# The low-part subtraction of a dense weight unit on GpSimd, as four instructions of 512 columns

## The chip, the cores and the metric

The kernel runs on one core of a Trainium2 chip. The metric is the device time of one execution in microseconds; the time before is 525.37 us, the median of three runs (525.44, 525.37, 520.17). Durations in the text come from one profiled execution, which took 521.39 us and whose span in the trace is 519.6 us. TensorE is the matrix engine (PE in the profile), VectorE is DVE, ScalarE is ACT, GpSimd is POOL, and SyncE (SP) issues most of the DMAs. SBUF is the on-chip memory of 128 partitions, PSUM the eight banks into which TensorE writes.

## What is computed

One layer of a hybrid decoder on 256 tokens of width 1024, all in float32:

```python
mod = silu(c) @ w_ada + b_ada                       # six vectors: sh1, sc1, gt1, sh2, sc2, gt2
h = rmsnorm(x, norm1) * (1 + sc1) + sh1
proj = h @ w_in                                     # 5640 columns, cut into
da_q, da_k, da_v, ml_qk, ml_v, ml_o, ml_if, g_a, g_m = split(proj)
y_a = diff_attention(da_q, da_k, da_v)              # 4 heads, causal, ALiBi, softmax1 - lam * softmax2
qk = silu(causal_conv(ml_qk, conv_w))               # 4 taps
h_t = mlstm(m_q, m_k, ml_v, gates)                  # 4 heads
y_m = rmsnorm(sigmoid(ml_o) * h_t)
merged = sigmoid(g_a) * (y_a @ w_br_a) + sigmoid(g_m) * (y_m @ w_br_m)
x = x + gt1 * (merged @ w_out)
h2 = rmsnorm(x, norm2) * (1 + sc2) + sh2
x = x + gt2 * hier_moe(h2)                          # 4 groups of 8 SwiGLU experts, top 1 group, top 2 experts
return rmsnorm(x, norm_f)
```

## The kernel before

The weights arrive in units of 128 partitions x 2048 columns (1 MB), each by one DMA of SyncE, into a ring of 8 slots. 54 units come before the experts: 24 of `w_ada` and 30 dense ones (`w_in`, the two branch projections, `w_out`; the list `DENSE`). SyncE loads unit n when TensorE has finished the job that used unit n - 8. The 96 units of the experts follow, through 16 slots, each load released by the matmuls that used its slot. The jobs of TensorE stand in the list `JOBS`, which also assigns the PSUM banks, eight in rotation; every engine's program is written out in order, and the engines meet by semaphores only.

A dense product is made in three passes of reduced-precision matmuls. Each factor is split into a high part (a rounded copy) and a low part (the value less its high part). For a weight unit, ScalarE writes the high part into one of three spare slots (`split`, L417 to L423, one instruction of 128x2048), once the unit has landed and the product three jobs earlier is done. It then counts up `w_hi`. GpSimd waits for that and subtracts the high part from the unit, in place in the ring, one instruction of 128x2048 per unit (L388), and counts up `w_lo`. It does nothing else but two memsets at the start. TensorE starts a product when `w_hi` says that the high part is there, runs eight matmuls of 128x256 with high times high, and waits for `w_lo` only before the pass that needs the low part (`product`, L1235 to L1247): the second pass where the weights are the stationary factor (`proj_T`), the third where they are the moving one (`proj`). A unit is 48 matmuls in all.

VectorE, meanwhile, does the small work of the layer. The parts of it that the text speaks of, in the order of its program:

- L765 and L768: the low part of the normalized input, two subtractions of 128x1024. TensorE's third pass of the gate projection and all that follows wait for L768.
- `scores(h)` (L812 to L816): scale and bias the attention scores out of a PSUM bank, and take row maxima.
- `combine(h)` (L822 to L827): from ScalarE's exponentials the difference of the two softmaxes, in SBUF.
- `conv(i)` (L835 to L841): the causal convolution, per 128-channel block one tensor_scalar (L835) and three scalar_tensor_tensor (L838), all in SBUF, each linked to the one before.
- The order is scores 0, scores 1, combine 0, scores 2, combine 1, scores 3, L701, conv 0, combine 2, L707 and L858, conv 1, combine 3, six small ones on the modulation vectors (L866 to L875), L879. L879 copies a PSUM bank, and by that frees the bank that TensorE needs for the `w_ada` product `ada(2)` (L1199).
- At the end of the dense stage, four pairs of L990 (a product out of a PSUM bank) and L992 (a sum in SBUF). ScalarE's L591 makes the high part of each merged quarter, and TensorE's output projection waits for the fourth.

Of the kernel before, what the change touches and what calls it, by code (L numbers as in the profile page):

```python
# [15 lines left out]
F32 = mybir.dt.float32  # L16
# [3 lines left out]
ALU = mybir.AluOpType  # L20
# [17 lines left out]
HI = 3  # L38
SLOTS = RING + HI + 1
UNIT = 2048  # L40


ROWS, NROWS = {}, 0
# [93 lines left out]
def build(nc, t, out):  # L137
    with ExitStack() as ctx:
        def sb(name, shape, dt=F32):
            return ctx.enter_context(nc.sbuf_tensor(name, [P] + list(shape), dt))  # L140

        def sem(name):
            return ctx.enter_context(nc.semaphore(name))

        def both(name, shape):

            with nc.sbuf_tensor(name + "_r", [P] + list(shape), F32R) as rounded:
                pass
            return sb(name, shape), rounded


        ring, ring_r = both("ring", [SLOTS, UNIT])
        const = sb("const", [NCONST])
# [137 lines left out]
        s = {n: sem(n) for n in names}  # L291
# [10 lines left out]
        def slot_of(n):  # L302

            return n % RING if n < NPRE + RING else n - NPRE
# [9 lines left out]
        def unit(n, k):  # L314

            return slot(slot_of(n)).rearrange("p (k n) -> p k n", k=k)

        def hi(d):

            return ring_r[:, RING + d % HI, :]  # L320
# [5 lines left out]
        def _(sp):  # L326
# [6 lines left out]
            for n, (kind, c0) in enumerate(UNITS):  # L333
# [6 lines left out]
                k = 4 if kind in ("br_a", "br_m") else 8  # L340
                w = UNIT // k
                sp.dma_start(unit(n, k), src[kind][:, :, c0:c0 + w]).then_inc(landed[slot_of(n)], 16)
# [38 lines left out]
        @block.gpsimd  # L381
        def _(pool):
            pool.memset(raw[:, :, 0:3], 0.0).then_inc(s["pads"], 1)
            pool.memset(vaug[:, :, :, P:P + 1], 1.0).then_inc(s["pads"], 1)

            for d, n in enumerate(DENSE):
                pool.wait_ge(s["w_hi"], d + 1)
                pool.tensor_tensor(ring_r[:, slot_of(n), :], ring[:, slot_of(n), :], hi(d).bitcast(F32),  # L388
                                   ALU.subtract).then_inc(s["w_lo"], 1)


        @block.scalar
# [782 lines left out]
        def _(pe):  # L1175
# [48 lines left out]
            def next_dense(k):  # L1224

                d = dense[0]
                dense[0] += 1
                n = DENSE[d]
                assert n == at[0]
                at[0] += 1  # L1230
                pe.wait_ge(s["w_hi"], d + 1)
                return hi(d).rearrange("p (k n) -> p k n", k=k), \
                    ring_r[:, slot_of(n), :].rearrange("p (k n) -> p k n", k=k), ((s["w_lo"], d + 1),)

            def product(out, a, b, nk):  # L1235

# [41 lines left out]
            for i in range(4):  # L1278
                ps = take(f"xT{i}")
                for j in range(2):  # L1280
                    for tt in range(TT):
                        k = 2 * i + j
# [13 lines left out]
            for i in range(4):  # L1296
                if i == 1:

                    ps = take("ifT")
                    pe.wait_ge(*free("if"))  # L1300
                    for g in range(2):
                        ins = pe.matmul(ps[0:4, g * T:(g + 1) * T], ident[0:8, 4 * g:4 * g + 4], grow[0:8, 2, :],
                                        start=True, stop=True)
                    filled(ins, "ifT")
                proj_T(f"qk{i}", hsrc, next_dense(8))
            ada(3)
            proj("v0", hsrc, next_dense(8))
            ada_turn(3)
            proj("v1", hsrc, next_dense(8))

            for i in range(4):
# [337 lines left out]
```

## Time and profile before

| | |
|---|---|
| median of three runs | 525.37 us |
| profiled execution, its own time | 521.39 us |
| its span in the trace | 519.6 us |
| TensorE (PE) busy | 432.9 us, 83% |
| ScalarE (ACT) busy | 173.9 us, 33% |
| VectorE (DVE) busy | 172.7 us, 33% |
| GpSimd (POOL) busy | 140.8 us, 27%, in 30 subtractions and six memsets |
| DMA | 163.19 MB, mean 314 GB/s, 422 GB/s in most of the last third |

How to read it: the span falls in a dense stage up to about 250 us, in which GpSimd works, a short routing stage, and the expert stage from about 295 us, in which it doesn't. A row that names an engine, a line and an operation gives the instructions issued at that line of the kernel; "<-" names what ended a wait. A VectorE or GpSimd row's length runs from issue to end and can hold time in which the instruction stood still. The granted clock of TensorE is a share of full speed: 0.5 is 1.2 GHz and 1.0 is 2.4 GHz.

### The profile page before, as it was taken

Reading aid. Unit: us, or ns where it says so; the run is one execution under the profiler, and the core shown is the slowest. Engines: PE = TensorE matmul, PEld = TensorE weight load, DVE = VectorE, ACT = ScalarE, POOL = GpSimd, SP = SyncE. Lnnn points to the kernel's source line nnn. Section 1 sums busy time; section 2 is a strip of 40 time slices with the busy share of each in tenths; the row PEclk is TensorE's granted clock in tenths of the full one; section 3 lists DMA queues with packets and bytes.
Section 4 is the critical chain, followed back from the end, with each engine's and each line's share of the span. In section 5 each row is a group of like instructions: output and inputs, shape, how many; then the busy total and the mean of one; then the engine's idle time right before and its main releaser. Section 6 shows DMA issues by size and latency. Waiting matters only on the chain.

```text
span 519.6 us, 8847 instructions
## 1 busy us (share of the span) xinstructions
PE 432.9 (83%) x3772; PEld 320.7 (62%) x3772; DVE 172.7 (33%) x345; ACT 173.9 (33%) x305; POOL 140.8 (27%) x36
## 2 busy tenths in 40 slices
PE   1846999999589999999896989898988859595883
PEld 0425988889559999998893654444544425261441
DVE  0245103899963524059326302111111110202013
ACT  1234531753327729452526330312121202020122
POOL 0009684655803673976510000000000000000000
PEclk9967999998879999999999898998989979999799
DMA  8999759487439726555959889999999999999952
GB/s 299 392 363 390 226 182 390 160 320 250 159 100 352 239 83 229 188 184 209 355 215 373 356 334 415 421 421 422 422 419 423 422 422 422 422 422 421 422 240 83
DMA packets 55718, 163.19 MB, mean 314 GB/s; under 512 B 7058, under 2 KB 33924, under 8 KB 43268
## 3 DMA queue, kind: packets, MB, share of 16 engines
q1 hardware_dynamic: 50528, 159.53, 79.6%
q10 hardware_dynamic: 5156, 3.17, 2.2%
q8 instruction: 25, 0.41, 0.3%
q14 instruction: 9, 0.07, 0.0%
HBM read 161.64 MB, written 1.05 MB: 313 GB/s over the span
## 4 chain that ended last, share of the span: by engine, by line
PE 55%; DMA 21%; DVE 15%; SPq 3%; ACT 3%; issue 2%; DVEq 0%
PE bank L1246 24%; DMA ring<-in_w_e 15%; PE bank L1555 8%; PE bank L1567 6%; PE bank L1528 5%; DMA ring<-in_w_ada 4%; PE bank L1517 4%; DVE mqk L838 3%; DMA ring<-in_w_in 2%; PE bank L1199 2%; DVE gm L992 2%; SPq L350 2%; DVE xn L827 1%; SPq L338 1%; DVE xn L825 1%
## 5 line engine op out<-in xcount | busy, mean ns | idle before, releaser
L388 POOL TENSOR_TENSOR ring_r<-ring,ring_r 128x2048 fp32r<-128x2048 f32 x30 | 140.4, 4688 | 120.3 <-ACT ring_r L423 120.3
L1246 PE MATMUL bank<-ring_r 128*128 128x256 f32 x832 | 112.5, 287 | 4.7 <-ACT ring_r L591 2.8
L1246 PEld LDWEIGHTS bank<-ring_r 128*128 128x128 f32 x832 | 105.4, 194 | 7.2 <-issue 3.9
L645 ACT ACTIVATE raw<-bank,sm 128x128 f32<-128x128 f32 x72 | 27.2, 458 | 163.2 <-PE bank L1528 163.2
L423 ACT ACTIVATE ring_r<-ring 128x2048 fp32r<-128x2048 f32 x30 | 57.3, 1911 | 41.2 <-PE bank L1246 26.2
L1555 PE MATMUL bank<-ring,raw 128*32 128x256 f32 x768 | 49.7, 401 | 12.5 <-DMA ring<-in_w_e 12.1
L1555 PEld LDWEIGHTS bank<-ring,raw 128*32 128x32 f32 x768 | 27.0, 115 | 32.6 <-issue 19.7
L1199 PE MATMUL bank<-ring,sm 128*32 128x256 f32 x384 | 29.2, 456 | 21.2 <-DMA ring<-in_w_ada 12.5
L1124 DVE TENSOR_TENSOR tmp<-bank,tmp 128x256 f32<-128x256 f32 x8 | 3.4, 425 | 127.2 <-ACT tmp L653 127.2
L1528 PEld LDWEIGHTS bank<-const,xn 128*128 128x128 f32 x288 | 35.7, 199 | 9.1 <-issue 7.1
L1567 PE MATMUL bank<-ring,WT 128*32 128x512 f32 x192 | 37.9, 650 | 3.5 <-DVE WT L1129 3.5
L1528 PE MATMUL bank<-const,xn 128*128 128x128 f32 x288 | 37.6, 286 | 1.1 <-DVE const L1075 1.1
L1246 PE MATMUL bank<-hT_r,ring_r 128*128 128x256 f32 x256 | 35.0, 280 | 0.0
L1199 PEld LDWEIGHTS bank<-ring,sm 128*32 128x32 f32 x384 | 12.8, 126 | 34.6 <-issue 10.9
L1517 PE MATMUL bank<-v,const 128*128 128x512 f32 x72 | 32.5, 593 | 1.7 <-DVE sm L1155 1.7
L1246 PEld LDWEIGHTS bank<-hT_r,ring_r 128*128 128x128 f32 x256 | 32.5, 190 | 0.0
L1567 PEld LDWEIGHTS bank<-ring,WT 128*32 128x32 f32 x192 | 10.0, 117 | 26.9 <-issue 24.1
L1135 DVE TENSOR_TENSOR v<-bank,att 128x512 f32<-128x512 f32 x16 | 10.3, 687 | 48.9 <-PE bank L1567 48.9
L1555 PE MATMUL bank<-hT,raw 128*32 128x256 f32 x64 | 17.6, 432 | 6.3 <-DMA mqk<-in_w_e 6.3
L1517 PEld LDWEIGHTS bank<-v,const 128*128 128x128 f32 x72 | 13.0, 190 | 15.5 <-issue 15.5
L838 DVE SCALAR_TENSOR_TENSOR mqk<-raw,cols,mqk 128x256 f32<-128x256 f32 x24 | 20.1, 836 | 0.9
L1246 PE MATMUL bank<-raw_r,ring_r 128*128 128x256 f32 x128 | 18.0, 282 | 0.0
(301 smaller groups left out, 549.7 us busy)
## 6 DMA issues: line engine op xcount, KB each, us to landing
ring<-in_w_e SPq DMA_DIRECT2D x72, 1024.0 KB, 22.5
ring<-in_w_ada SPq DMA_DIRECT2D x24, 1024.0 KB, 11.0
ring<-in_w_in SPq DMA_DIRECT2D x22, 1024.0 KB, 8.1
hT<-in_w_e SPq DMA_DIRECT2D x6, 1024.0 KB, 21.8
qkT<-in_w_e SPq DMA_DIRECT2D x6, 1024.0 KB, 23.7
gm<-in_w_e SPq DMA_DIRECT2D x6, 1024.0 KB, 24.9
mqk<-in_w_e SPq DMA_DIRECT2D x6, 1024.0 KB, 25.0
ring<-in_w_out SPq DMA_DIRECT2D x4, 1024.0 KB, 5.2
```

The lines of the kernel that those rows point to most:

```text
L350: sp.dma_start(slot(i), expert).then_inc(landed[i], 16)
L388: pool.tensor_tensor(ring_r[:, slot_of(n), :], ring[:, slot_of(n), :], hi(d).bitcast(F32), ALU.subtract).then_inc(s["w_lo"], 1)
L423: act.activation(hi(d), ring[:, slot_of(n), :], ACT.Copy).then_inc(s["w_hi"], 1)
L645: ins = act.activation(xg[:, b, k, :], token_bank[:, j * P:(j + 1) * P], ACT.Identity, bias=S("B2p", KD)[:, k:k + 1], scale=S("A2p", KD)[: ...
L838: ins = dve.scalar_tensor_tensor(out=mqk[:, k, :], in0=raw[:, k, j:j + T], scalar=col("conv_w", 8 * j + k), in1=mqk[:, k, :], op0=ALU.mult ...
L992: own(dve.tensor_tensor(va, va, view, ALU.add), "merged", i + 1)
L1199: ins = pe.matmul(ps[32 * u:32 * u + 32, 0:256], S("cs", 8)[:, k:k + 1].to_broadcast([P, 32]), w[:, k - k0, 256 * u:256 * u + 256], start= ...
L1246: ins = pe.matmul(out, left(k), right(k), start=(i == 0 and k == 0), stop=(i == 2 and k == nk - 1))
L1517: ins = pe.matmul(y_banks[2 * tt + c][:], ptg[:, b, tt, :], outs2[:, 512 * c:512 * c + 512], start=False, stop=stop, skip_group_check=True)
L1528: ins = pe.matmul(token_bank[:, j * P:(j + 1) * P], xn[:, tt, k * P:(k + 1) * P], pone[:, tt].rearrange("p a n -> p (a n)"), start=(tt == ...
L1555: ins = pe.matmul(up_bank[e * CAP:(e + 1) * CAP, half], xg[:, b, k, e * CAP:(e + 1) * CAP], wt[e][:, k, :], start=(k == 0), stop=(k == KD ...
L1567: ins = pe.matmul(out_banks[c][e * CAP:(e + 1) * CAP, :], hidT[:, f, e * CAP:(e + 1) * CAP], wt[e][:, f, 512 * c:512 * c + 512], start=(f ...
```

## The change

GpSimd's subtraction of a unit becomes four subtractions of 512 columns each, one after the other, each counting up `w_lo` by one. Only the first of the four has a wait (for `w_hi`). TensorE's wait for the low part of unit d goes from `w_lo >= d + 1` to `w_lo >= 4 * (d + 1)`, so it still waits for the whole unit. No other instruction of any engine changes or moves. The lines of the kernel behind each insertion shift: by one behind the constant, by three behind the loop, so that L388 is now L391 and VectorE's L768 is now L771.

```diff
@@ -38,6 +38,7 @@
 HI = 3
 SLOTS = RING + HI + 1
 UNIT = 2048
+PARTS = 4
@@ -385,8 +386,10 @@
             for d, n in enumerate(DENSE):
                 pool.wait_ge(s["w_hi"], d + 1)
-                pool.tensor_tensor(ring_r[:, slot_of(n), :], ring[:, slot_of(n), :], hi(d).bitcast(F32),
-                                   ALU.subtract).then_inc(s["w_lo"], 1)
+                for part in range(PARTS):
+                    sl = slice(part * UNIT // PARTS, (part + 1) * UNIT // PARTS)
+                    pool.tensor_tensor(ring_r[:, slot_of(n), sl], ring[:, slot_of(n), sl], hi(d)[:, sl].bitcast(F32),
+                                       ALU.subtract).then_inc(s["w_lo"], 1)
@@ -1230,7 +1233,7 @@
                 pe.wait_ge(s["w_hi"], d + 1)
                 return hi(d).rearrange("p (k n) -> p k n", k=k), \
-                    ring_r[:, slot_of(n), :].rearrange("p (k n) -> p k n", k=k), ((s["w_lo"], d + 1),)
+                    ring_r[:, slot_of(n), :].rearrange("p (k n) -> p k n", k=k), ((s["w_lo"], PARTS * (d + 1)),)
```

## Rows read from the trace of the kernel before

**Rows 1.** TensorE's waits, 36 to 250 us: engine line waited for: total us, times, longest

```profile
PE bank L1199 <- DVE sm L879: 8.7, 1, 8.7
PE bank L1246 <- DVE hT_r L768: 4.7, 1, 4.7
PE bank L1246 <- ACT ring_r L591: 2.8, 1, 2.8
```

**Rows 2.** the chain of waits in order of time: start us, us, what

```profile
39.80 4.79 DVE hT_r L768
...
127.10 4.72 DVE mqk L838
...
131.84 4.69 DVE mqk L838
...
145.32 5.50 PE bank L1199 x64
...
180.06 5.66 PE bank L1246 x48
...
234.85 3.59 DVE gm L992
...
239.20 4.93 DVE gm L992
...
248.94 1.10 PE bank L1246 x7
...
368.29 25.20 DMA ring<-in_w_e
```

**Rows 3.** VectorE by line, whole span: xcount: ns min/median/max, first and last start us

```profile
L838 DVE SCALAR_TENSOR_TENSOR mqk<-raw,cols,mqk x24: 483/485/4710, 114.1 to 158.6; 128x256 f32<-128x256 f32 x24
L825 DVE TENSOR_SCALAR xn<-att,sm x8: 285/316/4589, 99.3 to 137.5; 128x128 f32<-128x128 f32 x4, 128x256 f32<-128x256 f32 x4
L827 DVE SCALAR_TENSOR_TENSOR xn<-att,sm,xn x8: 352/419/4844, 99.6 to 142.1; 128x128 f32<-128x128 f32 x4, 128x256 f32<-128x256 f32 x4
L812 DVE SCALAR_TENSOR_TENSOR att<-bank,const x8: 536/548/558, 91.4 to 112.2; 128x384 f32<-128x384 f32 x8
```

**Rows 4.** timeline of VectorE and GpSimd, 97 to 118 us: start us, us, engine line operation

```profile
106.20 4.60 POOL L388 TENSOR_TENSOR ring_r<-ring,ring_r 128x2048 fp32r<-128x2048 f32 x1 [0.99 <-ACT ring_r L423]
106.24 4.84 DVE L827 SCALAR_TENSOR_TENSOR xn<-att,sm,xn 128x256 f32<-128x256 f32 x1
...
113.35 0.41 DVE L701 COPY arow<-bank 128x256 f32<-128x256 f32 x1
...
115.66 4.58 POOL L388 TENSOR_TENSOR ring_r<-ring,ring_r 128x2048 fp32r<-128x2048 f32 x1 [4.86 <-ACT ring_r L423]
115.69 4.71 DVE L835 TENSOR_SCALAR mqk<-raw,cols 128x256 f32<-128x256 f32 x1
```

**Rows 5.** GpSimd's L388 by line: whole span, then 40 to 48.9 us

```profile
L388 POOL TENSOR_TENSOR ring_r<-ring,ring_r x30: 4537/4610/5545, 37.9 to 257.0; 128x2048 fp32r<-128x2048 f32 x30
...
L388 POOL TENSOR_TENSOR ring_r<-ring,ring_r x2: 5539/5542/5545, 37.9 to 43.5; 128x2048 fp32r<-128x2048 f32 x2
```

**Rows 6.** GpSimd's timeline

```profile
0.79 0.11 POOL L384 MEMSET vaug<- 128x8 f32 x1
...
126.64 9.61 POOL L388 TENSOR_TENSOR ring_r<-ring,ring_r 128x2048 fp32r<-128x2048 f32 x2 [6.41 <-ACT ring_r L423]
...
207.54 18.45 POOL L388 TENSOR_TENSOR ring_r<-ring,ring_r 128x2048 fp32r<-128x2048 f32 x4 [6.38 <-ACT ring_r L423]
```

**Rows 7.** TensorE's timeline

```profile
71.88 3.66 PE L1199 MATMUL bank<-ring,sm 128*32 128x256 f32 x64
...
213.05 2.06 PE L1246 MATMUL bank<-ring_r 128*128 128x256 f32 x16
```

**Rows 8.** TensorE by stretch: from:to us, PE busy (x), granted clock, DMA share, GB/s

```profile
44.60:48.10 3.50, 3.47 (x17) 0.50 1.04 400
...
145.30:150.80 5.50, 5.48 (x65) 0.65 0.01 3
```

## The prediction

> **What bounds the kernel now.** I read the busy shares first, then TensorE's waits, then the chain of waits, and then VectorE beside GpSimd in the timeline. GpSimd does only one thing, 30 subtractions of 128x2048, and no engine is ever listed as having waited for them, so at first sight the edit touches nothing that counts. TensorE's waits between 36 and 250 us say otherwise: 8.7 us for L879, 4.7 us for L768 and 2.8 us for L591 [rows 1], and all three stand at the end of VectorE work. In the chain of waits VectorE's steps have lengths that their arithmetic doesn't explain: L838 takes 4.72 and 4.69 us, L992 3.59 and 4.93, L768 4.79 [rows 2]. Their normal lengths stand in the rows by line: L838 has a median of 485 ns and a maximum of 4710 for one and the same shape, L827 419 and 4844, L825 316 and 4589 [rows 3].
>
> The timeline shows what the long ones have in common [rows 4]. GpSimd's unit runs from 106.20 to 110.80 us; L827, issued at 106.24, ends at 111.08. The unit at 115.66 ends at 120.24; L835, issued at 115.69, ends at 120.40. So a VectorE instruction that reads SBUF alone (two SBUF tensors, or a tensor_scalar on one) stands still until GpSimd's running instruction ends. One that reads a PSUM bank doesn't: L812 stays between 536 and 558 ns in all its eight places [rows 3]. The reverse is there too: GpSimd's first two units took 5.54 us where 4.61 is the median [rows 5], because a 128x1024 subtraction of VectorE had the way first. The Trainium skill (SBUF — State Buffer, the section with the engine ports) calls this an exclusive lock on a shared port pair, held for the whole instruction by whichever starts first; by that rule, the trace agrees.
>
> What decides the edit is what happens **between two GpSimd instructions that are both ready**. There are two such places. The second unit was ready before the first ended at 43.49, yet L768 ran in between (to 44.59) and the second unit paid for it with its 5.54 us [rows 2, 5]. From 126.64 two units follow each other in 9.61 us, 0.4 more than twice 4.61 [rows 6], and an L838 got in at each end: 127.10 to 131.82, and 131.84 to 136.53 [rows 2]. VectorE's waiting instruction is let in at the boundary, one for one.
>
> **The change, part by part.**
>
> *GpSimd's own time.* One unit is 4.61 us; a quarter is 1.15 us plus a fixed part f. The bounds of f: nothing, or a whole small memset, 0.11 us [rows 6]. I take 0.05, so a part is 1.20 us and a unit 4.8. The cover: TensorE needs a unit per 5.66 us [rows 2], and wants the low part only after its first eight matmuls. The tightest place is the run of four units from 207.54: the first ends at 212.15, and TensorE starts on that job at 213.05 and has 0.9 us of work before it needs it [rows 6, 7], so 1.8 us are left. Even at f = 0.11, with a turn of VectorE (0.2 us, half of the 0.4 above) after each part, a unit grows by 1.2. Cost: 0. TensorE still waits for all four parts (its wait is multiplied by PARTS), so nothing starts earlier on that account. The 90 added semaphore increments release nobody: 0. [...]
>
> *First place, 39.8 us.* L768 is issued at 39.80. GpSimd, held up 0.93 us by the VectorE instruction before it (5.54 less 4.61), would end its first part at 37.95 + 0.93 + 1.2 = 40.1; L768 then needs its 1.1 us (44.59 less 43.49) and ends at 41.2 instead of 44.6. Gain 3.4 us, all on TensorE's path. The first unit's low part is ready at 40.1 + 0.9 + 3 x 1.2 = 44.6 instead of 43.5. TensorE wants it sixteen matmuls after 41.2; those take 3.5 us today [rows 8], so at 44.7: just in time, and the 3.4 stand.
>
> *Second place, 98 to 145 us.* TensorE waits 8.7 us, from 136.6 to 145.3, for L879, the last of a long VectorE queue [rows 1, 2]. I walk through that queue with parts of 1.2 us, GpSimd's units starting where they do now, since they wait for ScalarE's splits, and these for TensorE and for transfers that TensorE's releases start. At 106.24 L827 waits for one part instead of four: it ends at 107.7 instead of 111.08. Six score instructions and a copy (111.1 to 113.7 today, [rows 4]) need no port and run beside the rest of that unit, to 110.3; the first conv instruction, L835, meets its last part and ends at 111.4 instead of 114.1. The other seven of conv 0, at 0.5 us [rows 3], end at 114.9, before the unit at 115.66, which today stops an L835 for 4.3 us. The combine behind it (1.9 us: two each of L825 and L827 and two tiny ones) meets that unit and takes turns with its parts: it ends at 119.6; today at 120.4 + 1.5 + 1.9 = 123.8. Conv 1 ends at about 125.0, before the unit at 126.64; today two of its instructions are stopped there and it ends at 136.5. The last combine ends at 126.8. The eight short instructions to L879 take turns with the parts where they need the port (five do, at most 1.2 us each) and end near 133.3. TensorE arrives at 136.6: the whole 8.7 us goes, with 3.3 us to spare. A second effect follows. After the idle stretch the granted clock is 0.65 and the 64 matmuls of L1199 take 5.50 us; the same 64 take 3.66 at 71.88, where TensorE came to them busy [rows 2, 7, 8]. That is 1.8 us more. Together 10.5 us. What is late next there: TensorE's own work.
>
> *Third place, 234 to 249 us.* L992 waits 2.9 and 4.2 us (3.59 and 4.93, less its 0.7) for two units [rows 2]. With parts, the four pairs L990/L992 end at 236.2, 239.0, 242.7 and about 245.4, and the last L591 at 246.0; TensorE ends its own work at 246.1 (248.94 less 2.8). Gain 2.7 us of 2.8.
>
> *Elsewhere.* An instruction of VectorE that today comes just behind a unit's end can meet the longer unit: a loss of 0.2 us (4.8 less 4.61), taken once. After 250 us GpSimd has two units and nothing waits. The expert transfers (25.20 us in one piece of the chain at 368.29, [rows 2]) are issued when TensorE frees buffers, so they move with it, and the end moves as much as the start.
>
> **Sum:** 3.4 + 10.5 + 2.7 - 0.2 = 16.4 us. The profiled execution took 521.39 us, so 505.0. It is 4.0 us under the median of the three runs, 525.37, two of which are at 525.4; I put half of that on top: **507 us**.
>
> **Rivals.**
>
> *A, VectorE pays in instalments.* Its instructions that need the port follow each other within 30 ns, so each meets the next part, and a unit costs it the same 4.6 us in four pieces; only what needs no port is gained. For it: the combine above already behaves so, and if conv 1 slips past 126.64 it meets 9.6 us of GpSimd again. Against it: the 3.3 us to spare. Then the second place keeps only the 3.4 us won at 106.24 and half of the clock, 0.9, and the third 1.4: 3.4 + 3.4 + 0.9 + 1.4 = 9.1 us, 512.3, or 516.3 beside runs like the two at 525.4. Chance 0.17.
>
> *B, the parts don't open the port.* Four instructions with no wait between them could run as one block, GpSimd taking the port for the next part before it lets the last go. Then nothing changes: 521 to 526 us. Against it: VectorE got in between two ready units both times there were two. For it: those were whole units with a wait of their own in front. The Trainium skill (GPSIMD Engine Reference, instruction dispatch) says that a core starts instruction N+1 as soon as its share of N is done, with no barrier between, which could have this result. Chance 0.10.
>
> *C, slower: a part costs far more than a quarter.* Its place is TensorE's wait for the low part in the two runs of back-to-back projections, some 14 units. It begins at f = 0.26 us (4 x 1.41 = 5.66, the pace); with 4 us of slack in each run it uses up the gain at f = 0.7 (7.4 us a unit, 14 x 1.75 = 24.5 = 8 + 16.4), and at f = 0.9, 8.2 us a unit, the time would be 521.4 + 14 x 2.55 - 8 - 16.4 = 533. Only the memset speaks to f, and it speaks against this. Chance 0.05. That leaves 0.68 for the forecast's own case.
>
> **The numbers.** About 1% is what a measurement can tell here, so the bounds are 520.1 and 530.6. Faster: the forecast and nearly all of A, 0.84. Same: B and what is left of A, 0.11. Slower: C, 0.05. The range: below, all idle time gone, the clock restored in the first place too (0.5 there, [rows 8], about 2 us), and a median like the fastest run, gives 500; above, A beside the slower runs with the clock effect missing, 518.
>
> **What would show it.** L838, L825, L827 and L992 with maxima near 1.7 us instead of 4.7, but more instances above the median; GpSimd's 120 parts at 1.15 to 1.25 us, some at 1.4 to 2.1 where VectorE went first; TensorE's wait for L768 near 1.3 us, those for L879 and L591 gone; the L1199 after 136 us at 3.6 us per 64. Maxima that stay at 4.7 would be B; TensorE waiting for GpSimd's subtraction would be C; a wait of 3 to 5 us for L879 would be A. The forecast is wrong if the expert transfers don't move with the start of the expert stage.

## The result, and the profile after

The changed kernel takes **506.89 us** (median of 4 executions, 506.11 to 508.67), the kernel before, beside it, 523.08 (520.17 to 525.44). The ratio is 0.969, with a 95% interval of 0.965 to 0.974: faster by 3.1%. Here and below, ratios and intervals are taken from the executions within 1.5% of their kernel's fastest, while medians and ranges in us are of all its executions. The profiled execution took 506.75 us, its span is 505.0 and its mean granted clock 0.948; before it was 521.39, 519.6 and 0.936. So between the two profiled executions, against which the prediction's sum was made, there are **14.6 us**. The forecast for the profiled one was 505.0, for the median 507.

TensorE's waits between 36 and 250 us, as in [rows 1] (engine line waited for: total us, times, longest):

```profile
PE bank L1249 <- ACT ring_r L444: 2.6, 1, 2.6
PE bank L1249 <- DVE att L815: 2.3, 1, 2.3
PE bank L1249 <- POOL ring_r L391: 1.6, 1, 1.6
PE bank L1249 <- DVE hT_r L771: 1.5, 1, 1.5
PE bank L1249 <- ACT ring_r L594: 0.7, 1, 0.7
```

Line numbers have grown by three: L768 is L771, L838 is L841, L879 is L882, L591 is L594. The wait of 8.7 us for L879 is gone, 4.7 has become 1.5, 2.8 has become 0.7. One wait is new: 1.6 us for GpSimd's subtraction. L444's and L815's stood before as well and are not the change's.

GpSimd and VectorE by line, as in [rows 3, 5] (count: ns min/median/max, first and last start in us):

```profile
L391 POOL TENSOR_TENSOR ring_r<-ring,ring_r x120: 1263/1294/2285, 37.7 to 244.3; 128x512 fp32r<-128x512 f32 x120
L841 DVE SCALAR_TENSOR_TENSOR mqk<-raw,cols,mqk x24: 483/485/1384, 108.1 to 145.5; 128x256 f32<-128x256 f32 x24
L828 DVE TENSOR_SCALAR xn<-att,sm x8: 286/812/1393, 94.7 to 122.7; 128x128 f32<-128x128 f32 x4, 128x256 f32<-128x256 f32 x4
L830 DVE SCALAR_TENSOR_TENSOR xn<-att,sm,xn x8: 350/885/1395, 96.0 to 123.0; 128x128 f32<-128x128 f32 x4, 128x256 f32<-128x256 f32 x4
L995 DVE TENSOR_TENSOR gm<-gm,mqk x4: 1057/1308/1637, 220.5 to 230.7; 128x512 f32<-128x512 f32 x4
```

The maxima of L838, L825 and L827, 4.7, 4.6 and 4.8 us before [rows 3], are 1.4 now (L841, L828, L830): one part and not one unit. L995, which is the L992 of before, is at 1.64. The medians of L828 and L830 have risen (316 to 812 ns, 419 to 885 ns), since in this execution more of their instances meet a part. The minima stand: the instructions themselves cost what they did, and a stop costs less.

GpSimd's timeline (start us, us, operation, count, idle before):

```profile
37.74 22.22 POOL L391 TENSOR_TENSOR ring_r<-ring,ring_r 128x512 fp32r<-128x512 f32 x16 [36.83 <-ACT ring_r L426]
...
79.40 5.02 POOL L391 TENSOR_TENSOR ring_r<-ring,ring_r 128x512 fp32r<-128x512 f32 x4 [2.87 <-ACT ring_r L426]
...
112.00 5.10 POOL L391 TENSOR_TENSOR ring_r<-ring,ring_r 128x512 fp32r<-128x512 f32 x4 [4.13 <-ACT ring_r L426]
122.74 10.75 POOL L391 TENSOR_TENSOR ring_r<-ring,ring_r 128x512 fp32r<-128x512 f32 x8 [5.64 <-ACT ring_r L426]
...
193.06 38.17 POOL L391 TENSOR_TENSOR ring_r<-ring,ring_r 128x512 fp32r<-128x512 f32 x28 [5.85 <-ACT ring_r L426]
```

An undisturbed unit takes 5.02 us, against 4.61: 0.41 more over four parts, 0.10 us a part. The parts' own lengths say 1.29 us each, and four of them make 5.16, not 5.02: a part's length in the trace reaches about 0.04 us into the next one. VectorE's timeline over the second combine:

```profile
111.98 1.39 DVE L828 TENSOR_SCALAR xn<-att,sm 128x128 f32<-128x128 f32 x1
113.41 1.28 DVE L830 SCALAR_TENSOR_TENSOR xn<-att,sm,xn 128x128 f32<-128x128 f32 x1
114.62 1.36 DVE L828 TENSOR_SCALAR xn<-att,sm 128x256 f32<-128x256 f32 x1
116.01 1.37 DVE L830 SCALAR_TENSOR_TENSOR xn<-att,sm,xn 128x256 f32<-128x256 f32 x1
...
123.03 1.40 DVE L830 SCALAR_TENSOR_TENSOR xn<-att,sm,xn 128x256 f32<-128x256 f32 x1
124.35 1.50 DVE L869 TENSOR_TENSOR tmp<-arow,const 128x256 f32<-128x256 f32 x1
...
128.59 1.21 DVE L878 SCALAR_TENSOR_TENSOR sm<-sm,pcol 128x8 f32<-128x8 f32 x1
129.72 0.16 DVE L882 COPY sm<-bank 128x16 f32<-128x16 f32 x1
```

The unit from 112.00 stops four instructions in a row, each for the part that runs. All four together wait about as long as one did for a whole unit, and GpSimd's unit takes 5.10 us instead of 5.02: being let in costs it next to nothing. From 122.74 three are stopped for most of a part (L830, L869 and L878), two more (L875 and L877) for 0.3 us each, and L882 ends at 129.88. TensorE gets to the product that needs its bank at 132.87, and finds it free. TensorE's timeline (a bracket is the idle time before and what ended it):

```profile
41.16 1.10 PE L1249 MATMUL bank<-hT_r,w_if_hi 128*8 128x256 f32 x8 [1.47 <-DVE hT_r L771]
42.09 1.10 PE L1249 MATMUL bank<-ring_r 128*128 128x256 f32 x8
44.78 1.22 PE L1249 MATMUL bank<-ring_r 128*128 128x256 f32 x8 [1.58 <-POOL ring_r L391]
...
132.87 3.66 PE L1202 MATMUL bank<-ring,sm 128*32 128x256 f32 x64
...
232.50 1.22 PE L1249 MATMUL bank<-ring_r 128*128 128x256 f32 x8 [0.73 <-ACT ring_r L594]
...
269.41 3.78 PE L1531 MATMUL bank<-const,xn 128*128 128x128 f32 x16 [1.08 <-DVE const L1078]
272.98 3.05 PE L1604 MATMUL bank<-x,const 128*128 128x512 f32 x4
...
280.24 3.66 PE L1558 MATMUL bank<-ring,raw 128*32 128x256 f32 x64 [0.39 <-issue]
```

The 64 matmuls after L882 take 3.66 us, 5.50 before [rows 2]; the granted clock there is 1.00, and was 0.65 [rows 8]. Where the 14.6 us arise is read from the moments at which TensorE reaches the same instruction in both traces:

| TensorE reaches | before, us | after, us | earlier by | of this new |
|---|---|---|---|---|
| its first product after L768/L771 | 44.63 | 41.16 | 3.5 | 3.5 |
| the end of the gate work (L1302/L1305) | 53.76 | 49.68 | 4.1 | 0.6 |
| the first product after L812/L815 | 92.07 | 88.41 | 3.7 | -0.4 |
| L1199/L1202, held by L879/L882 | 145.32 | 132.87 | 12.5 | 8.8 |
| its end | 150.75 | 136.46 | 14.3 | 1.8 |
| the output projection, held by L591/L594 | 248.94 | 232.50 | 16.4 | 2.1 |
| the gather of tokens (L1528/L1531) | 285.87 | 269.41 | 16.5 | 0.0 |
| the first expert product (L1555/L1558) | 295.50 | 280.24 | 15.3 | -1.2 |
| the end of the span | 519.6 | 505.0 | 14.6 | -0.7 |

### The profile page after: what moved, and what is told of

It reads as the page before. It is cut to its first block, busy times and chain, and to the rows that moved or that the text cites. A ratio compares the mean times of both kernels' runs of the same rounds, so it can differ in the third digit from the quotient of the medians.

```text
span 505.0 us, 8937 instructions
## 1 busy us (share of the span) xinstructions
PE 426.5 (84%) x3772; PEld 319.0 (63%) x3772; DVE 159.5 (32%) x345; ACT 173.7 (34%) x305; POOL 157.3 (31%) x126
## 4 chain that ended last, share of the span: by engine, by line
PE 62%; DMA 24%; DVE 4%; SPq 3%; ACT 2%; issue 2%; POOL 1%; DVEq 0%; ACTq 0%
PE bank L1249 33%; DMA ring<-in_w_e 15%; PE bank L1558 8%; DMA mqk<-in_w_e 5%; PE bank L1570 4%; PE bank L1531 4%; DMA ring<-in_w_ada 4%; PE bank L1520 3%; PE bank L1202 3%; SPq L351 2%; SPq L339 1%; POOL ring_r L391 1%; PE bank L1604 1%; PE bank L1486 1%; ACT ring_r L426 1%
## 5 line engine op out<-in xcount | busy, mean ns | idle before, releaser
L391 POOL TENSOR_TENSOR ring_r<-ring,ring_r 128x512 fp32r<-128x512 f32 x120 | 156.9, 1345 | 87.8 <-ACT ring_r L426 87.6
L1249 PE MATMUL bank<-ring_r 128*128 128x256 f32 x832 | 111.3, 285 | 4.6 <-DVE att L815 2.3
L1249 PEld LDWEIGHTS bank<-ring_r 128*128 128x128 f32 x832 | 103.8, 191 | 7.3 <-issue 4.3
L1558 PE MATMUL bank<-ring,raw 128*32 128x256 f32 x768 | 51.9, 423 | 17.3 <-DMA ring<-in_w_e 16.9
L1558 PEld LDWEIGHTS bank<-ring,raw 128*32 128x32 f32 x768 | 28.3, 121 | 39.5 <-issue 27.8
L1531 PEld LDWEIGHTS bank<-const,xn 128*128 128x128 f32 x288 | 35.9, 199 | 9.0 <-issue 7.8
L1531 PE MATMUL bank<-const,xn 128*128 128x128 f32 x288 | 37.7, 286 | 1.1 <-DVE const L1078 1.1
L1202 PE MATMUL bank<-ring,sm 128*32 128x256 f32 x384 | 27.3, 434 | 12.3 <-DMA ring<-in_w_ada 12.3
L1570 PE MATMUL bank<-ring,WT 128*32 128x512 f32 x192 | 32.3, 595 | 3.5 <-DVE WT L1132 3.5
L1202 PEld LDWEIGHTS bank<-ring,sm 128*32 128x32 f32 x384 | 12.3, 120 | 24.3 <-DMA ring<-in_w_ada 9.4
L1138 DVE TENSOR_TENSOR v<-bank,att 128x512 f32<-128x512 f32 x16 | 10.3, 685 | 42.7 <-PE bank L1570 42.7
L1570 PEld LDWEIGHTS bank<-ring,WT 128*32 128x32 f32 x192 | 8.9, 109 | 22.5 <-issue 19.6
L1558 PE MATMUL bank<-hT,raw 128*32 128x256 f32 x64 | 16.9, 418 | 5.5 <-DMA mqk<-in_w_e 5.5
L1558 PE MATMUL bank<-qkT,raw 128*32 128x256 f32 x64 | 16.9, 418 | 0.0
## 6 DMA issues: line engine op xcount, KB each, us to landing
ring<-in_w_ada SPq DMA_DIRECT2D x24, 1024.0 KB, 10.8
```

The source lines that it names most:

```text
L391: pool.tensor_tensor(ring_r[:, slot_of(n), sl], ring[:, slot_of(n), sl], hi(d)[:, sl].bitcast(F32), ALU.subtract).then_inc(s["w_lo"], 1)
L1138: ins = dve.tensor_tensor(outs2[:, sl], out_banks[c][:], gt2b[:, sl], ALU.mult)
L1202: ins = pe.matmul(ps[32 * u:32 * u + 32, 0:256], S("cs", 8)[:, k:k + 1].to_broadcast([P, 32]), w[:, k - k0, 256 * u:256 * u + 256], start= ...
L1249: ins = pe.matmul(out, left(k), right(k), start=(i == 0 and k == 0), stop=(i == 2 and k == nk - 1))
L1531: ins = pe.matmul(token_bank[:, j * P:(j + 1) * P], xn[:, tt, k * P:(k + 1) * P], pone[:, tt].rearrange("p a n -> p (a n)"), start=(tt == ...
L1558: ins = pe.matmul(up_bank[e * CAP:(e + 1) * CAP, half], xg[:, b, k, e * CAP:(e + 1) * CAP], wt[e][:, k, :], start=(k == 0), stop=(k == KD ...
```

## The experiments

Twelve kernels ran, in three groups, each group beside its own runs of the kernel before (medians 524.7, 524.3 and 522.4 us; the single executions scatter from 519.6 to 528). Ratios are to those. PARTS as a list means so many parts for unit d, with the slices and TensorE's count (the sum of the list so far) to match. Each kernel has one trace, so waits and lengths are those of one execution.

### The three places one at a time, and units 0 to 14 together

```diff
-PARTS = 4
+PARTS = [4 if d == 0 else 1 for d in range(30)]          # first place alone
+PARTS = [4 if 8 <= d <= 14 else 1 for d in range(30)]    # second place alone
+PARTS = [4 if 24 <= d <= 27 else 1 for d in range(30)]   # third place alone
+PARTS = [4 if d <= 14 else 1 for d in range(30)]         # first, second, and units 1 to 7
```

> Only the first of the 30 units is cut in four; the other 29 stay whole. Theory (shared port, three places that add up): L768 ends at about 41.2 instead of 44.6, TensorE waits 1.5 us for it instead of 4.7 and passes the point at 53.8 us about 3.5 to 4 us earlier; the waits of 8.7 us for L879 and 2.8 us for L591 stay. Time about 4 us under the kernel before, ratio near 0.993. Rival (the gain comes from GpSimd's units being short everywhere, or from a restored clock, and not from single places): no more than 1/30 of the 16 us, 0.5 us, ratio 0.999.

> Only units 8 to 14 are cut in four, the seven that run while VectorE works through scores, combine and conv. Theory: TensorE's wait of 8.7 us for L879 goes and the 64 matmuls of L1199 behind it take 3.7 instead of 5.5 us; the waits of 4.7 and 2.8 us stay. Time 10.5 us lower, ratio near 0.980. Rival (VectorE pays for the parts one by one, the gain needs the shift from the first place too): 4 to 6 us, ratio 0.990.

> Only units 24 to 27 are cut in four, those beside the pairs L990/L992. Theory: TensorE's wait for L591 falls from 2.8 to about 0.7 us, the start of the expert stage comes 2.1 us earlier, and the end by 2 us or, where the expert stage is held by its transfers, whose first four are issued before this wait, by less, 1 us. Ratio 0.996 to 0.998. Rival (the transfers alone set the end of the expert stage): 0 us, ratio 1.000.

> Units 0 to 14 are cut in four, 15 to 29 stay whole. With units 8 to 14 alone cut, TensorE still waited 3.4 us for L879, because VectorE came to conv 1 and the third combine some 2 us later against GpSimd's units than in the changed kernel, and all five of the combine's instructions took turns with parts. Theory (what counts is where VectorE's bursts fall between the units; cutting units 0 to 7 moves them): as in the changed kernel, VectorE is done with L879 before TensorE asks, the wait is gone, L1199 takes 3.7 us; only the third place stays, 2.8 us for L591. Time 2 to 3 us over the changed kernel, 509 to 510. Rival (the places are independent of each other): the waits of the middle-only kernel, 3.4 us and the slow L1199 behind it, 2.5 us, come back: 515.

| in parts | median, us (executions) | ratio, interval | TensorE's wait for L771, us | for L882 | for L594 |
|---|---|---|---|---|---|
| none (before) | - | 1 | 4.7 | 8.7 | 2.8 |
| first | 520.6 (12) | 0.992, 0.988 to 0.996 | 1.5 | 8.9 | 2.8 |
| second | 519.9 (10) | 0.987, 0.982 to 0.993 | 5.1 | 3.4 | 2.8 |
| third | 520.4 (12) | 0.993, 0.990 to 0.996 | 4.7 | 8.8 | 0.7 |
| units 0 to 14 | 507.3 (4) | 0.976, 0.969 to 0.983 | 1.7 | 0 | 2.8 |
| all (the change) | 506.9 (4) | 0.969, 0.965 to 0.974 | 1.5 | 0 | 0.7 |

The first and the third place alone shorten their own waits as they were said to. In time they give 0.8% and 0.7%; for the third 0.2 to 0.4% was expected. The traces don't show these gains at the end: their two spans are 520.3 and 519.9 us, against 519.6 before. With the first place alone, what was gained is lost again behind the wait for L594, where TensorE's clock is lower in that trace; with the third alone, it is lost mostly in the gather of tokens. Both are taken up under "What follows the dense stage" and "The median" below. **The second place doesn't do what was said of it**: 0.987 came, 0.980 was expected. With whole units up to d = 7, VectorE comes to the last combine when GpSimd's pair of units has already begun, and meets a part with every instruction. Timelines of VectorE and of GpSimd with the second place alone:

```profile
126.38 1.05 DVE L826 TENSOR_SCALAR sm<-sm 128x2 f32<-128x2 f32 x1
127.46 1.27 DVE L828 TENSOR_SCALAR xn<-att,sm 128x128 f32<-128x128 f32 x1
128.77 1.29 DVE L830 SCALAR_TENSOR_TENSOR xn<-att,sm,xn 128x128 f32<-128x128 f32 x1
129.98 1.38 DVE L828 TENSOR_SCALAR xn<-att,sm 128x256 f32<-128x256 f32 x1
...
132.71 1.50 DVE L869 TENSOR_TENSOR tmp<-arow,const 128x256 f32<-128x256 f32 x1
```

```profile
124.46 10.89 POOL L391 TENSOR_TENSOR ring_r<-ring,ring_r 128x512 fp32r<-128x512 f32 x8 [4.69 <-ACT ring_r L426]
```

GpSimd's pair starts at 124.46 and VectorE's combine at 126.18, 1.7 us after it. In the changed kernel the combine starts at 121.59 and the pair at 122.74; with units 0 to 14 in parts, 119.98 and 121.76. There most of the combine runs free before the pair. Cutting units 0 to 7 as well moves GpSimd's pair by 2.7 us (124.46 to 121.76) and VectorE's last combine by 6.2. Of the 6.2, 4.1 are there from the first combine on (96.59 to 92.44), and the other 2.1 come on the way to the last one. Along that way two groups of three L841 run free (1.53 us each), where with the second place alone they are stopped (3.35 and 2.44). So what the second place gives depends on where VectorE stands when the units come. Whether unit 0 alone would have moved it as far, or units 1 to 7 are what counts, wasn't tried. What is left with the second place alone costs more than itself, in TensorE's timeline:

```profile
138.71 6.20 PE L1202 MATMUL bank<-ring,sm 128*32 128x256 f32 x64 [3.44 <-DVE sm L882]
```

6.20 us for the 64 matmuls, against 3.66 without the wait. The first and the second place alone give 0.8% and 1.3%, units 0 to 14 at once 2.4%. The intervals are too wide to tell 2.1 from 2.4; the wait that is 3.4 us in one trace and gone in the other tells it. The third place, put on top of units 0 to 14, takes TensorE's wait for L594 from 2.8 to 0.7 us, but the medians, 507.3 and 506.9, don't tell the two kernels apart (509 to 510 was expected for the first).

### One, two, four, eight parts

```diff
-PARTS = 4
+PARTS = 2
```

> Each unit in two parts of 1024 columns, about 2.35 us each. Theory (a VectorE instruction waits at most for the running part): longest waits 2.4 us instead of 4.7 and 1.3; L768 ends at about 42.4, so the first place gives 2.2 us; in the middle place two thirds of the gain, TensorE waits 2 to 4 us for L879; time 511 to 514. Rival (any boundary at all is enough, since VectorE needs only to be let in once per unit): as the changed kernel, 507.

```diff
-PARTS = 4
+PARTS = 8
```

> Each unit in eight parts of 256 columns. The fixed part read from the changed kernel is 0.10 us (1.255 from start to start, less 1.153), so a part is 0.68 us and a unit 5.4, against TensorE's pace of 5.66. Theory: the blocked instructions of VectorE now last 0.7 to 1.1 us, but what they held up on TensorE's path is already gone; the first low part comes 0.3 us later; the changed kernel's time within 1 us, 506 to 508. Rival 1 (finer is better, the remaining waits scale with the part): 504. Rival 2 (GpSimd falls behind the pace, and TensorE waits for low parts in the runs of projections): 510 to 515, with waits for GpSimd's line above 3 us.

Two parts give 512.5 us (507.7 to 518.0, 4 runs), ratio 0.980 (0.970 to 0.990): waits of 2.7 us for L771, 1.9 for L882, 1.3 for L594. Four have 3.7 us less of these waits and 1.4 less in L1202's matmuls (5.05 against 3.66), but 1.6 more for GpSimd's subtraction. That is 3.5 us net, of 4.5 between the two profiled executions (511.29 and 506.75) and 5.6 between the medians. **Eight parts undo the whole gain**: 526.0 us (518.1 to 527.9, 10 runs), ratio 0.998 (0.991 to 1.003), which none of the theories had. GpSimd's own price is small; its subtractions by line and its timeline:

```profile
L391 POOL TENSOR_TENSOR ring_r<-ring,ring_r x240: 712/738/1754, 38.1 to 266.1; 128x256 fp32r<-128x256 f32 x120
```

```profile
38.14 29.79 POOL L391 TENSOR_TENSOR ring_r<-ring,ring_r 128x256 fp32r<-128x256 f32 x40 [37.23 <-ACT ring_r L426]
73.36 16.62 POOL L391 TENSOR_TENSOR ring_r<-ring,ring_r 128x256 fp32r<-128x256 f32 x24 [5.44 <-ACT ring_r L426]
...
105.40 12.06 POOL L391 TENSOR_TENSOR ring_r<-ring,ring_r 128x256 fp32r<-128x256 f32 x16 [7.21 <-ACT ring_r L426]
...
201.54 33.25 POOL L391 TENSOR_TENSOR ring_r<-ring,ring_r 128x256 fp32r<-128x256 f32 x48 [5.27 <-ACT ring_r L426]
```

48 parts in 33.25 us are 0.69 us each, a unit 5.5 us, just under TensorE's pace of 5.66 [rows 2], and TensorE waits for it only 0.5 us. The waits of TensorE that cost the time are others:

```profile
PE bank L1249 <- DVE qkT_r L969: 10.7, 1, 10.7
PE bank L1320 <- DVE v L794: 3.6, 1, 3.6
```

and VectorE's timeline shows what made them:

```profile
52.42 15.64 DVE L783 TENSOR_SCALAR o<-o 4x256 f32<-4x256 f32 x1
...
84.45 5.57 DVE L793 COPY sm<-sm 128x8 f32<-128x8 f32 x1
...
107.59 0.72 DVE L828 TENSOR_SCALAR xn<-att,sm 128x128 f32<-128x128 f32 x1
...
145.41 3.02 DVE L838 TENSOR_SCALAR mqk<-raw,cols 128x256 f32<-128x256 f32 x1
...
216.61 19.34 DVE L969 TENSOR_TENSOR qkT_r<-qkT,raw_r 128x512 fp32r<-128x512 f32 x2 [17.98 <-ACT raw_r L586]
```

A tensor_scalar on four partitions stands still for 15.6 us. It is stopped at 52.42 and ends at 68.06, and GpSimd's run of 40 parts ends at 67.93; the L793 copy ends at 90.0 with the run of 24 that began at 73.36, and the first of the two L969 takes 18.7 us, to 235.3, where the run of 48 ends at 234.8. Here the parts do **not** open the port: between two of them GpSimd keeps it, and VectorE gets in only when GpSimd has nothing ready. Yet at 107.59 another tensor_scalar, between parts of the same size, is let in after 0.72 us. The four instructions shut out came 14.3, 11.1, 14.1 and 15.1 us after GpSimd's unbroken run had begun; those let in at such a boundary came at the latest 10.6 us after it. But with four parts to a unit an L969 was let in 15 us into the run of 28 (208.13, within the run from 193.06), so the depth alone isn't the rule. What decides is open. All of this is read from one execution (525.86 us); whether the faster ones of this kernel had the same stops isn't known.

### GpSimd made to wait between its parts

```diff
                 for part in range(PARTS):
+                    if part:
+                        pool.wait_ge(s["w_lo"], PARTS * d + part)
```

> Eight parts, and GpSimd waits before each part but the first for its own previous one to be counted. With eight parts and no such waits, VectorE was shut out for 15.6, 19.3 and 5.6 us in three places, while each part of GpSimd started 0.03 to 0.06 us before the one before it had ended. Theory (a part that starts before the last has ended can keep VectorE out; only a real gap opens the port each time): no VectorE instruction above 1.6 us, and TensorE's waits of 10.7 us for L969 and 3.6 us for L794 gone. The gaps cost about 0.1 us each, so a unit takes 6.2 us or more, over TensorE's pace of 5.66, and TensorE begins to wait for low parts: 508 to 516, below the 526 without the waits. Rival (256 columns are too short a part whatever stands between them): VectorE is shut out as before, 525 or more.

> The changed kernel, and GpSimd waits before parts 2 to 4 of a unit for its own previous part. Theory: with four parts VectorE was let in at almost every boundary already, so nothing is gained there; a unit takes 5.3 to 5.5 us instead of 5.02, the first low part comes 0.3 to 0.4 us later; 507 to 508. Rival (the overlap of parts cost something in the changed kernel too): under 506.

A wait on its own last count stands between each part and the next. With eight parts this takes the time from 526.0 us (ratio 0.998) to 512.65 us (512.0 to 514.9, 4 runs), ratio 0.981 (0.976 to 0.987), though GpSimd is slower by it. In its timeline (the first eight units):

```profile
36.94 53.65 POOL L393 TENSOR_TENSOR ring_r<-ring,ring_r 128x256 fp32r<-128x256 f32 x64 [36.04 <-ACT ring_r L428]
```

6.7 us a unit, over TensorE's pace, so TensorE waits 4.1 us for it in four places. And VectorE's L785, which is the L783 above, in the same place, 16 us after that row's start:

```profile
53.35 0.68 DVE L785 TENSOR_SCALAR o<-o 4x256 f32<-4x256 f32 x1
```

0.68 us instead of 15.64, and no VectorE instruction takes over 1.8 us. That **shows** that a wait between the parts ends the shutting-out. It doesn't show by what: the wait also makes the parts slower, and with four parts VectorE is let in without it. With four parts, the same wait makes a unit 5.38 us and the time 510.8 (509.5 to 514.8, 4 runs), ratio 0.979 (0.973 to 0.985); 507 to 508 was expected. It isn't needed there, and it costs some 1% of the time. Part of that is a new wait of TensorE for L884, which is L882, in its timeline:

```profile
133.74 5.35 PE L1204 MATMUL bank<-ring,sm 128*32 128x256 f32 x64 [0.92 <-DVE sm L884]
```

0.9 us waited, 1.7 us longer matmuls. At the third place TensorE now waits 1.5 us, for the subtraction L988 (L986 of the changed kernel), where it waited 0.7 for L594.

### What is left, and what a part costs

```diff
-            for d, n in enumerate(DENSE):
-                pool.wait_ge(s["w_hi"], d + 1)
-                ...
-                    ring_r[:, slot_of(n), :]...., ((s["w_lo"], PARTS * (d + 1)),)
+                    hi(d).rearrange("p (k n) -> p k n", k=k), ()
```

> GpSimd subtracts nothing, and the pass with a unit's low part multiplies its high part again: same matmuls, no GpSimd work, no wait for w_lo. This gives the floor of what the port costs. Theory: VectorE's instructions are all at their medians; against the changed kernel 1.6 us of TensorE's wait for the first low part, some 0.9 us at L768, 0.5 us at L812 and 0.7 us at L591 go as well, so 3 to 4 us under the changed kernel, near 503. Rival (VectorE still pays much of the port time on TensorE's path after the change): 496 or lower. If the expert stage is set by its transfers, 505.

Measured: 503.65 us (502.8 to 504.4, 4 runs), ratio 0.960 (0.953 to 0.967). This kernel leaves the low part of the weights out of its products, so it doesn't compute the layer; it is a bound and no candidate. With no GpSimd beside it VectorE still lets TensorE wait 1.2, 1.5 and 1.3 us. By this, GpSimd's subtractions cost the kernel before some 21 us in all, and 3.2 are left in the changed one. Not all of the 3.2 is the port: TensorE's wait of 1.6 us for the first low part went as well.

```diff
-                    pool.tensor_tensor(...).then_inc(s["w_lo"], 1)
+                    ins = pool.tensor_tensor(...)
+                ins.then_inc(s["w_lo"], 1)
```

> The changed kernel, but only the last of the four parts counts up w_lo, and TensorE waits for d + 1 as before the change. It tells whether the fixed part of 0.10 us belongs to the count or to the instruction. Theory (to the instruction): parts still 1.25 us from start to start, time as the changed kernel, 507. Rival (to the count, GpSimd draining each part for it): parts at 1.16 us, a unit at 4.65, and TensorE's wait for the first low part 0.3 us shorter; or, if it is the draining that lets VectorE in, VectorE instructions of 4 us and more come back and the time is 515 or more.

507.04 us (506.9 to 508.7, 4 runs), ratio 0.971 (0.965 to 0.976). GpSimd by line:

```profile
L391 POOL TENSOR_TENSOR ring_r<-ring,ring_r x120: 1257/1293/2297, 38.4 to 244.9; 128x512 fp32r<-128x512 f32 x120
```

1293 ns where it was 1294: the count costs nothing, the 0.10 us belong to the instruction. VectorE's longest instruction is 1.77 us in both kernels, so it isn't the count that lets VectorE in.

### TensorE waits for each part

```diff
     for k in range(nk):
+        if low is not None and (k == 0 or -(-(k + 1) * PARTS // nk) != -(-k * PARTS // nk)):
+            pe.wait_ge(s["w_lo"], low - (-(k + 1) * PARTS // nk))
```

> The changed kernel, and TensorE waits before each pair of matmuls of the low-part pass only for the part that they read, instead of for all four. Theory: of the 1.6 us that TensorE waits for the first unit's low part 0.8 is won, since the last part still comes at 44.7 and only two matmuls stand behind it; no other unit is waited for; 506 us, within noise of the changed kernel. Rival (added waits in TensorE's queue cost issue time, some 90 more semaphore waits): 508 or more.

507.53 us (505.7 to 509.4, 4 runs), ratio 0.974 (0.968 to 0.980). The wait for the subtraction falls from 1.6 to 0.7 us; the time can't tell it from the change.

### The parts only where they pay, with that wait

```diff
-PARTS = 4
+PARTS = [4 if d <= 14 or 24 <= d <= 27 else 1 for d in range(30)]
```

> Units 0 to 14 and 24 to 27 in four parts, the others whole, and TensorE waiting for each part only before the matmuls that read it. It joins what each run showed to count: the three places, and 0.8 us at the first low part. Theory: 505.5 to 506.5, at most 1 us under the changed kernel and within its noise, since the floor without GpSimd's work is 503.65. Rival (whole units 15 to 23 put VectorE back behind TensorE near L907 and L969): 508 to 510.

507.21 us (506.5 to 509.1, 6 runs), ratio 0.971 (0.967 to 0.975): the same again. No version that computes the layer is told from the change as faster.

## Why the prediction was right, and where it was off

**What is held, and how it is let in.** Right. VectorE's maxima are one part (1.4 us, L995 1.64; said: near 1.7), the medians of L828 and L830 rose, and VectorE is let in at every boundary. Rival B, that the parts don't open the port, didn't happen here, but it is real: it is what eight parts do. The prediction set it aside on two boundaries between whole units, and those could not tell. That parts of 512 columns let VectorE in, where parts of 256 didn't, was luck as far as the prediction's reasons go. The Trainium skill (GPSIMD Engine Reference, instruction dispatch) says that each of GpSimd's cores goes on to the next instruction without a barrier between. The traces fit that: the lengths of the parts overlap by 0.04 us, VectorE is shut out for up to 18 us with eight, and a wait between the parts ends it. Why four parts, whose lengths overlap as well, let VectorE in is open.

**GpSimd's own time.** f was taken as 0.05 us a part and is 0.10, within the bounds of 0 to 0.11. A unit is 5.02 us and not 4.8. The cover held except at the first unit, where TensorE waits 1.6 us.

**First place, 3.4 us forecast.** 4.1 came, 0.2 of it there from the start (GpSimd's first part begins at 37.74, its first unit of before at 37.95), and by another sum than the one written. L771 ended as said: TensorE's product after it starts at 41.16, forecast 41.2. Then two errors cancel. TensorE was to need the low part after sixteen matmuls in 3.5 us; that length was taken at the clock of 0.50 [rows 8]. In the profiled execution the granted clock is 1.00 from 41.1 us on, after 0.63 in the 5 us before, and eight of them take 1.10 us, from 42.09. So TensorE arrives earlier and waits 1.6 us for GpSimd, which the step had "just in time". The clock gained more than the wait costs, by 0.6 us. That the clock came back is not owed to the shorter wait alone: after waits of 1.5, 1.6 and 1.5 us for the same instruction the first eight matmuls took 1.88 us, as before the change, with the first place alone, with eight parts, and with four parts and the own wait. The 1.6 can be cut to 0.7 (a wait per part), which the time doesn't show.

**Second place, 10.5 us.** 8.8 and 1.8, 10.6 in all: right to 0.1 us. The walk through the queue had 3.3 us to spare, and TensorE arrives 3.0 after L882's end. But the prediction treated the places as independent, and they aren't. Alone, the second place keeps 3.4 us of wait and 2.5 of slow matmuls; that is rival A, VectorE paying in instalments, under the condition that the prediction gave it: the queue slips past the start of the pair of units (conv 1 ends at 126.25 us, the pair starts at 124.46). In the changed kernel the last combine starts 1.1 us ahead of it, and rival A doesn't come.

**Third place, 2.7 us.** 2.1 came. The pairs L993/L995 end later than forecast, L594 by about as much: 0.7 us of wait remain where 0.1 was said. From the first L993 to the end of the last L995 it took 12.0 us, forecast 11.3. All four L995 were stopped, two of them by most of a part (1.64 us at most), and GpSimd's unit is longer than the 4.8 assumed. The step also left out VectorE's L986 (L983 before), the low part of each merged quarter, which stands between the pairs. It ran free before, at 0.69 us; now two of them are stopped, for 1.8 us together:

```profile
225.13 1.57 DVE L986 TENSOR_TENSOR gm_r<-gm,ring_r 128x512 fp32r<-128x512 f32 x1
...
228.43 1.66 DVE L986 TENSOR_TENSOR gm_r<-gm,ring_r 128x512 fp32r<-128x512 f32 x1
```

Which of the three made the 0.6 us wasn't tried.

**Elsewhere, -0.2 us.** It was -0.4, at one place: the wait for L812/L815 went from 1.9 to 2.3 us, since the tiny L793 just before it was stopped by a part.

**What follows the dense stage, 0 us.** This is the term that was furthest off: it was -1.9. The prediction said that the end moves as much as the start. It does nearly so from the first expert product on: from there to the end of the span it is 224.1 us before and 224.8 after, and 224.0 to 224.7 in the twelve other kernels. Before it, 1.2 us are lost in the gather, where the clock was lower in the execution after. The same two groups took less before:

```profile
285.87 3.56 PE L1528 MATMUL bank<-const,xn 128*128 128x128 f32 x16 [1.08 <-DVE const L1075]
289.26 1.88 PE L1601 MATMUL bank<-x,const 128*128 128x512 f32 x4
```

3.78 and 3.05 us after, at a granted clock of 0.58 from 269.4 to 276.5; before, 0.72 from 285.8 to 291.5. From the start of the gather to the first expert product it is 9.6 us before and 10.8 after. In the five traces with a wait of 0.7 to 0.8 us for L594, the changed kernel's among them, it is 10.3 to 10.8, and in eight with another wait or none 9.6 to 9.8; but with the second place alone, whose wait is 2.8 us, it is 10.8. So part of the third place's gain may be lost here through the clock. With one trace of each kernel that isn't shown. Sum of what was and wasn't foreseen: 4.1 - 0.4 + 10.6 + 2.1 - 1.2 - 0.7 = 14.5, and 14.6 with rounding.

**The median.** 507 was reached from 505.0 by adding half of the 4 us between the profiled execution and the median of before. The kernel before scatters in two groups, near 521 and near 525.5 (29 runs beside the first experiments span 519.6 to 527.4); the change's four runs lie within 2.6 us. The 2 us were nearly right by luck: the profiled execution was 1.8 us over its forecast, and the median 0.1 over the profiled one. Where the two groups come from wasn't tried. One thing that can make them is seen in the traces. With the first place alone, the 144 matmuls after the 2.8 us wait for L594 take 20.06 us, at a clock of 0.85; after the same wait they take 17.35 at 1.00 in the kernel before. With the second place alone they start as slowly as with the first: the first eight take 2.08 us, against 1.21. A kernel with fewer waits would then scatter less; that is argued, not shown.

## What to carry to other kernels

When a long instruction of one engine stops short ones of another, its length is the price of each stop, and the stops end up as waits of an engine that uses neither: look for one form with a median of 0.5 us and a maximum of ten times that, and for a partner whose start and end fit. Cutting the long instruction into parts pays here because its engine has a fifth of the pace to spare where it is tightest (4.61 us of 5.66), and the cut has an optimum: halves leave waits, eighths bring the whole loss back unless a wait stands between them. And a place that is cured alone may pay little where what comes earlier decides what meets what: try it together with the others before giving it up.

## What the runs showed that was not expected

- VectorE can be kept out over many instruction boundaries: up to 18 us by parts of 0.69 us, and in no trace here by parts of 1.26 us or by whole units. A semaphore wait between the parts ended it, for about 1 us a unit (from 5.5 us to between 6.4 and 6.9).
- Short idle stretches of TensorE can cost more than themselves. The 64 matmuls of L1202 after 130 us take 3.66 us in every trace without a wait, and 5.35, 5.05, 6.20 and 5.54 us after waits of 0.9, 1.9, 3.4 and 8.9 us: the surcharge of 1.4 to 2.5 us doesn't grow with the wait. It isn't so everywhere: after the wait of 2.8 us for L594 the next eight matmuls take 1.21 us in the kernel before and 2.08 with the first place alone.
- An instruction of GpSimd costs 0.10 us beyond its columns when the next one is ready, with or without a semaphore count, and lengths in the trace overlap by 0.04 us.
